# Scan of four head pairs: token buffers in two head layouts, and modulation panels in four column groups

## The chip, the cores and the metric

The kernel runs on one core of a Trainium2 chip. The metric is the device time of one execution in microseconds; the median of three runs is given, and one execution was recorded by the hardware profiler. The core's engines work side by side and meet at semaphores: PE (matmuls; PEld are its weight loads), DVE (VectorE), ACT (ScalarE), POOL (GpSimd), and SP, which issues the loads.

## What is computed

The reference is two transformer blocks on 512 tokens of width 1024. The first mixes tokens with a retention group and an RWKV-7 group (8 heads of 64), then has a mixture of experts; the second has dilated attention, a gated convolution and MLPs. The change lies in the RWKV group of the first block:

```
def rwkv7_scan(r, w, k, v, a, b, s0):
    def step(S, inp):
        r_t, w_t, k_t, v_t, a_t, b_t = inp
        sa = jnp.einsum('bhvk,bhk->bhv', S, a_t)
        S = S * w_t[:, :, None, :] + sa[..., None] * b_t[:, :, None, :] + v_t[..., None] * k_t[:, :, None, :]
        return S, jnp.einsum('bhvk,bhk->bhv', S, r_t)
...
yc_f, sc_f = rwkv7_scan(rc, wc_f, kc, vc, ac, bc, s0)
yc_b, sc_b = rwkv7_scan(*[flip(t) for t in (rc, wc_b, kc, vc, ac, bc)], s0)
y_f, _ = rwkv7_scan(r, w_f, k, v, a, b, sc_f)
y_b, _ = rwkv7_scan(*[flip(t) for t in (r, w_b, k, v, a, b)], sc_b)
lat = g_f * (rwkv_group_norm(y_f, lnx_w, lnx_b) + bonus) + g_b * (rwkv_group_norm(flip(y_b), lnx_w, lnx_b) + bonus)
```

It runs forwards and backwards, over 256 context tokens and then the 512 tokens. The modulation vectors `silu(c) @ w_mod + b_mod` are needed later and are computed in the same stretch.

## The kernel before

The scan is done in blocks of 64 tokens (`CH`), NB = 12 blocks (4 of context, 8 of the rest), so that the step-by-step recurrence becomes 64x64 products. `rwkv_scan` (L1470) runs four times, once for each pair of heads; "scan 1" to "scan 4" below are these. Head 0 of the pair lies on partitions 0 to 63, head 1 on 64 to 127. For each direction d (0 forwards, 1 backwards) the work is a row of named jobs, `pe_jobs`; one job is 24 products (2 heads x 12 blocks) in float32, each written as one call that becomes two weight loads and two matmuls, so 48 matmuls. `both_heads` (L1534) gives the order: head 0 and head 1 in turn, into different PSUM banks. Since a head's inputs and its outputs lie on the same 64 partitions, a job uses the quarter of the array with rows and columns 0 to 63 and the one with rows and columns 64 to 127.

The jobs: SB, SK, SR are scores; KT, BT, AT, V turn an operand; MT is the masked SB, to which an identity is added on DVE (L1738, L1740), M0 its transpose on PE (L1600); AKV is a product. Then come the solver's levels: T1, M1, N1, T2, ... N3, T4, (AT), N4. T multiplies a mask level E (POOL, L1870) by M; ACT copies T out; M and N multiply by T, and DVE adds them to M and MT (L1759). N(lv) needs T(lv), not M(lv). After them XA, XV, ZA, ZV, YA, YV (products, L1552), G, H, RP, and the ten state steps S1 to S10 (L1668 on PE, L1780 on DVE), each of which needs the one before; Y is the output. PE runs a job for d = 0, then for d = 1, then the next job. Three PSUM regions of two banks go round over the list `turns`: a job first waits for the eviction of the job three turns earlier (`bank_free`). KT, M0, BT, AKV, T, AT, XA, XV, ZA, ZV, Y are emptied by ACT (L1826), the rest by DVE; both take orders strictly in the order written.

Between the jobs stand pieces of other work: `RwkvPrep` prepares the next pair (scans 1 to 3; on DVE after MT, N1, N2, N3, N4), and `RwkvOut` finishes the previous pair (scans 2 to 4): `sums` after AT, `square_sums` after ZA, `gates` after YA on PE, and `finish` (L1398) on DVE after YV, seven operations of 512 columns that wait for one another. `ModPanels` (L1412) makes a quarter of the modulation panels of the second half in each scan: 4 panels x 8 slices = 32 units. A unit multiplies a slice of `silu` (2 columns) by 256 columns of weights as two products of 128 columns in two column groups (partitions 0 and 64 of the output, L1435). Eight units stand between RP and S1, the other 24 between the state steps. `keep` (ACT) and `transpose` (PE, after the first Y) bring them into place.

Of the kernel before, what the change touches and what calls it, by code (L numbers as in the profile page):

```python
# [21 lines left out]
ALU = mybir.AluOpType  # L22
# [3 lines left out]
P = 128  # L26
# [1299 lines left out]
class RwkvOut:  # L1326
# [71 lines left out]
    def finish(self, dve):  # L1398

        V, y, step = self.nc.vector, self.y, self.step  # L1400
        for d in range(2):
            dve.wait_ge(self.rooted, d + 1)
            step.link(dve, V.scalar_tensor_tensor(y[:, d], y[:, d], self.col("lnx_w"), self.sq[:, d], ALU.mult, ALU.mult))
            step.link(dve, V.scalar_tensor_tensor(y[:, d], y[:, d], self.col("lnx_b"), self.f.bonus, ALU.add, ALU.add))
            dve.wait_ge(self.gated, d + 1)
            step.link(dve, V.tensor_tensor(y[:, d], y[:, d], self.banks[2][d][:], ALU.mult))
        dst = self.latT[:, 4 + self.hp, :].rearrange("c (j p) -> c p j", j=NT)
        a, b = (y[:, d].rearrange("c (p j) -> c p j", j=NT) for d in range(2))
        step.link(dve, V.tensor_tensor(dst, a, b, ALU.add))


class ModPanels:  # L1412
# [3 lines left out]
    def __init__(self, nc, g, hp, rows, banks):  # L1416
# [8 lines left out]
        self.part = banks[0][0:66].rearrange("r (n c) -> r n c", n=self.n_panel)  # L1425
        self.turn = [b[:, 0:2 * self.n_panel].rearrange("p (n c) -> p n c", c=2) for b in (banks[1], banks[0])]

    def rows_of(self, pe, lo, hi):

        for u in range(lo, hi):  # L1430
# [3 lines left out]
            for i, h in enumerate(self.halves):  # L1434
                last = self.nc.tensor.matmul(self.part[h, n], self.g.silu[:, k, :], self.w[:, k, i * P:(i + 1) * P], start=(k == 0), stop=(k == KD - 1))  # L1435
# [34 lines left out]
def rwkv_scan(nc, g, hp, f, tri, prep_of, out_of):  # L1470
# [20 lines left out]
    pe_jobs = ["SB", "SK", "SR", "KT", "M0", "BT", "AKV", "T1", "M1", "N1", "T2", "M2", "N2", "T3", "M3", "N3", "T4", "AT", "N4",  # L1491
               "XA", "XV", "ZA", "ZV", "YA", "YV", "G", "H", "RP"] + states + ["Y"]
    dve_jobs = ["SB", "SK", "SR", "MT", "M1", "N1", "M2", "N2", "M3", "N3", "N4", "YA", "YV", "G", "H", "RP"] + ["S0"] + states
    act_jobs = ["KT", "M0", "BT", "AKV", "T1", "T2", "T3", "T4", "AT", "XA", "XV", "ZA", "ZV", "Y"]

    with ExitStack() as tmp, nc.Block() as block:
# [23 lines left out]
        mods = ModPanels(nc, g, hp, f.Y[0:66, 1].rearrange("r (n c) -> r n c", c=P), prep_banks)  # L1520
        st, p0 = g.stream, g.stream.taken
        n_unit = KD * mods.n_panel
        turns = [("SB", 0), ("SK", 0), ("SB", 1), ("SK", 1), ("SR", 0), ("KT", 0), ("SR", 1), ("KT", 1), ("V", 0)]
        turns += [(job, d) for job in pe_jobs[4:] for d in range(2)]
        region = {turn: i % 3 for i, turn in enumerate(turns)}
        head = lambda h: slice(HD * h, HD * (h + 1))
# [3 lines left out]
        eye = lambda h: g.ident[head(h), head(h)]  # L1530
        halves = [slice(0, NB // 2), slice(NB // 2, NB)]
# [11 lines left out]

        @block.tensor
        def _(pe):
# [26 lines left out]
            def run(name, d):  # L1572
                bank_free(name, d)
                if name == "SB":
                    for h, s in both_heads(NB // 2):
                        last = mm(cell(d, name, h, s, NB // 2), f.Bh[head(h), d, chunk(s)], f.A[head(h), d, chunk(s)], start=True, stop=True)
# [15 lines left out]
                elif name == "AT":  # L1592
                    dve(d, "N3")
                    last = turn(name, d, f.A[:, d])
                elif name == "M0":
                    dve(d, "MT")
                    if d == 0:
                        pe.wait_ge(v_turned, 1)
                    for h, s in both_heads(NB // 2):
                        last = mm(cell(d, name, h, s, NB // 2), MT[d][head(h), s], eye(h), start=True, stop=True)  # L1600
                elif name == "AKV":
                    act(d, "BT")
                    pe.wait_ge(v_turned, 1)
                    for h, s in both_heads(NB // 2):
                        last = mm(cell(d, name, h, s, NB // 2), AK[d][head(h), s], Vt[head(h), s], start=True, stop=True)
                elif name[0] == "T":
# [6 lines left out]
                    last = product(name, d, E[lv % 2], M)  # L1613
                elif name[0] == "M":
# [6 lines left out]
                    last = product(name, d, MT, T1)  # L1621
                elif name[0] == "N":
# [4 lines left out]
                    last = product(name, d, T1, MT)  # L1627
                elif name == "XA":
                    act(d, "AT")
                    dve(d, "N4")  # L1630
                    last = product(name, d, MT, At)
                elif name == "XV":
                    dve(d, "N4")
                    last = product(name, d, MT, WV)
                elif name == "ZA":
                    pe.wait_ge(pool_done[d], LV)
                    act(d, "XA")
                    last = product(name, d, E[LV % 2], XA)
                elif name == "ZV":
                    act(d, "XV")  # L1640
                    last = product(name, d, E[LV % 2], XV)
                elif name == "YA":
                    act(d, "ZA")
                    last = product(name, d, MT, T1)
                elif name == "YV":
                    act(d, "ZV")
                    last = product(name, d, MT, ZV)
                elif name == "G":
                    dve(d, "YA")
                    last = product(name, d, XA, Bt)  # L1650
# [1977 lines left out]
```

## Time and profile before

| | |
|---|---|
| median of 3 runs | 3154.09 us (3149.6 to 3159.63) |
| the profiled execution | 3149.06 us |
| its span, first to last instruction | 3146.9 us |
| PE busy | 2876.5 us, 91% |
| DVE / ACT / POOL busy | 1134.7 / 942.3 / 778.9 us |
| mean granted TensorE clock | 0.963 |
| scans 1 to 4 (from the first SB to the next scan) | 117.6, 130.9, 131.0, 126.0 us |

In the rows below a time is a start in microseconds from the span's start, then the length. Consecutive instructions of one form are merged into one row (x96 is 96 of them). "idle before <- releaser" is how long the engine had stood still and what ended it; "issue" and "PEq" mean that nothing in the profile but PE's own sequencer was waited for. Some matmul records are missing, so a count may be a few short. A granted clock of 1.00 is 2.4 GHz and 0.50 is 1.2 GHz.

### The profile page before, as it was taken

The page shows a single profiled execution, that of the slowest core. Times are in us where ns is not written, and L with a number is a line of the kernel's source. Part 1 is how long each engine was busy: PE and PEld are TensorE (multiplying, and loading weights), DVE is VectorE, ACT ScalarE, POOL GpSimd, SP SyncE. Part 2 cuts the span into 40 slices and gives each one's busy share as a digit, 9 for nine tenths or more (in the row PEclk, how much of TensorE's full clock was granted, in tenths as well). Part 3 has the DMA queues.
Part 4 walks back from the last instruction along what each step waited for, and adds up shares of the span by engine and source line. Part 5 has one row for each costly group of instructions (what it writes and reads, how often), then busy time and mean ns, then how long its engine had stood idle before and what let it go on. Part 6 is the DMA issues. An engine that isn't in the chain of part 4 may idle for free. (4 is left out here: it accounts for less than half of the span.)

```text
span 3146.9 us, 54449 instructions
## 1 busy us (share of the span) xinstructions
PE 2876.5 (91%) x24397; PEld 2238.6 (71%) x24397; DVE 1134.7 (36%) x1676; ACT 942.3 (30%) x1586; POOL 778.9 (25%) x218
## 2 busy tenths in 40 slices
PE   6987999999967898998899999997999989899998
PEld 4765888887855432333489989986788868678887
DVE  3434764654354300110455447363211123421111
ACT  3123233433323100000235554553322222132221
POOL 3320321220211000000132223222344424334442
PEclk8989999999988899999999999998999999999999
DMA  6111201011122599999521322222232223223321
GB/s 252 54 31 39 67 17 59 4 58 57 45 89 80 216 427 427 427 426 427 224 95 54 81 68 78 70 68 80 69 105 94 94 69 105 69 80 100 102 94 54
DMA packets 171627, 397.57 MB, mean 126 GB/s; under 512 B 9551, under 2 KB 99636, under 8 KB 146036
## 3 DMA queue, kind: packets, MB, share of 16 engines
q1 hardware_dynamic: 170416, 390.70, 33.9%
q8 instruction: 193, 3.16, 0.4%
q10 hardware_dynamic: 980, 3.40, 0.3%
q14 instruction: 38, 0.31, 0.0%
HBM read 387.71 MB, written 4.19 MB: 125 GB/s over the span
## 5 line engine op out<-in xcount | busy, mean ns | idle before, releaser
L179 POOL TENSOR_TENSOR weight_ring_lo<-weight_ring,weight_hi 128x2048 fp32r<-128x2048 f32 (+1 forms) x144 | 657.6, 4568 | 1995.6 <-ACT weight_hi L168 1956.3
L168 ACT CAST weight_hi<-weight_ring 128x2048 fp32r<-128x2048 f32 (+1 forms) x144 | 271.0, 1884 | 671.5 <-PE mlp_o L213 247.3
L213 PE MATMUL a_o<-weight_hi,latT_hi 128*128 128x512 f32 x576 | 176.7, 429 | 2.5 <-PEq L3325 2.5
L213 PE MATMUL a_o<-weight_ring_lo,latT_hi 128*128 128x512 f32 x576 | 158.2, 397 | 0.0
L213 PE MATMUL a_o<-weight_hi,latT_lo 128*128 128x512 f32 x576 | 157.7, 396 | 0.0
L1870 POOL TENSOR_TENSOR rws_E<-rws_AT,rw_tri 128x768 f32<-128x768 f32 x40 | 76.3, 1931 | 322.4 <-DVE rws_AT L1750 209.6
L213 PE MATMUL mlp_o<-weight_hi,mlp_hid_hi 128*128 128x512 f32 x512 | 138.8, 393 | 9.8 <-issue 9.8
L3201 DVE TENSOR_TENSOR x<-x,mlp_o 128x512 f32<-128x512 f32 x64 | 44.0, 687 | 281.4 <-PE mlp_o L213 281.4
L213 PEld LDWEIGHTS a_o<-weight_hi,latT_hi 128*128 128x128 f32 x576 | 133.0, 273 | 16.8 <-issue 8.2
L213 PEld LDWEIGHTS a_o<-weight_ring_lo,latT_hi 128*128 128x128 f32 x576 | 134.2, 270 | 8.1
L213 PEld LDWEIGHTS a_o<-weight_hi,latT_lo 128*128 128x128 f32 x576 | 134.2, 270 | 7.8
L3186 DVE TENSOR_TENSOR mlp_hid<-mlp_hid,mlp_h 128x512 f32<-128x512 f32 x64 | 41.2, 685 | 272.8 <-ACT mlp_hid L3161 272.8
L213 PE MATMUL mlp_o<-weight_ring_lo,mlp_hid_hi 128*128 128x512 f32 x512 | 138.4, 393 | 0.0
L213 PE MATMUL mlp_o<-weight_hi,mlp_hid_lo 128*128 128x512 f32 x512 | 137.1, 390 | 0.0
L204 PE MATMUL mlp_h<-latT_hi,weight_hi 128*128 128x512 f32 x512 | 129.4, 396 | 4.8 <-PEq L3325 4.8
L2405 ACT ACTIVATE moe_silu<-moe_t 128x256 f32<-128x256 f32 x32 | 12.3, 384 | 388.1 <-PE moe_t L2364 387.2
L204 PE MATMUL mlp_h<-latT_lo,weight_hi 128*128 128x512 f32 x512 | 128.3, 393 | 0.0
L204 PE MATMUL mlp_h<-latT_hi,weight_ring_lo 128*128 128x512 f32 x512 | 126.5, 389 | 0.0
L2348 PE MATMUL moe_gu<-weight_ring,moe_xsT 128*64 128x512 f32 x248 | 111.8, 596 | 11.9 <-DMA weight_ring<-in_w_up 6.8
L213 PEld LDWEIGHTS mlp_o<-weight_hi,mlp_hid_hi 128*128 128x128 f32 x512 | 96.9, 190 | 30.6 <-issue 10.5
L2349 PE MATMUL moe_gu<-weight_ring,moe_xsT 128*64 128x512 f32 x256 | 116.2, 598 | 0.0
L204 PEld LDWEIGHTS mlp_h<-latT_hi,weight_hi 128*128 128x128 f32 x512 | 97.6, 191 | 25.7 <-issue 5.4
(617 smaller groups left out, 5801.7 us busy)
## 6 DMA issues: line engine op xcount, KB each, us to landing
weight_ring<-in_mlp_w SPq DMA_DIRECT2D x64, 1024.0 KB, 5.1
weight_ring<-in_a_wqkv SPq DMA_DIRECT2D x36, 1024.0 KB, 5.1
weight_ring<-in_w_up SPq DMA_DIRECT2D x32, 1024.0 KB, 20.3
weight_ring<-in_w_gate SPq DMA_DIRECT2D x31, 1024.0 KB, 22.1
weight_ring<-in_w_down SPq DMA_DIRECT2D x31, 1024.0 KB, 21.6
weight_ring<-in_w_mod SPq DMA_DIRECT2D x24, 1024.0 KB, 5.3
weight_hi_spare<-in_w_up SPq DMA_DIRECT2D x12, 1024.0 KB, 19.9
weight_hi_spare<-in_w_gate SPq DMA_DIRECT2D x12, 1024.0 KB, 22.3
```

The costliest lines, as they stand in the source:

```text
L168: self.nc.scalar.copy(self.view(self.hi[:, q % 2], p, True), self.view(self.slots[self.slot[p]], p, True)).then_inc(self.hi_ready, 1)
L179: self.nc.gpsimd.tensor_tensor(self.view(self.lo[:, s], p, True), self.view(self.slots[s], p, True), self.view(self.hi[:, q % 2], p, True) ...
L204: last = nc.tensor.matmul(dst, left(a, k), right(b, k), start=(a + b + k == 0), stop=(a == 1 and k == KD - 1))
L213: last = nc.tensor.matmul(dst, left(a, HK * r + k), right(b, k), start=(r + a + b + k == 0), stop=(r == 1 and a == 1 and k == HK - 1))
L1870: nc.gpsimd.tensor_tensor(E[lv % 2][d][:], AT[d][:], tri[:, 2 + lv, d].unsqueeze(1).to_broadcast([P, NB, CH]), ALU.mult).then_inc(pool_don ...
L2348: x = nc.tensor.matmul(acc[e % 2][h][0:CAP, :], xsT[:, k, tokens], wg[:, r, cols(h)], start=(k == 0), stop=(k == KD - 1))
L2349: y = nc.tensor.matmul(acc[e % 2][h][CAP:P, :], xsT[:, k, tokens], wu[:, r, cols(h)], start=(k == 0), stop=(k == KD - 1))
L2405: nc.scalar.activation(silu[:, i], turn[i][:, :, 0:CAP], ACT.Silu).then_inc(silued, 1)
L3186: last = V.tensor_tensor(d, d, up[i % 2][h][:], ALU.mult)
L3201: last = V.tensor_tensor(d, d, acc[j][:], ALU.add)
```

## The change

Four things are done.

1. Each 64x64 buffer of a pair is kept in one of three layouts, given as (partition half, slot) for head h and block s: `own` (as before), `left` (head on its own half, blocks of even and odd number in different slots) and `right` (blocks of odd number on the other head's half). With left inputs a product can write a right output and the reverse, so that of four neighbouring products each uses another quarter of the array (`four_tiles`). This holds for M0, AKV, T1 to T4, M1 to M3, AT, XA, XV, ZA, ZV, YA, YV. N1 to N4 and SB stay with two quarters (`two_tiles`), and so do SK, SR, KT, BT, V, G, H, RP and Y in the old order.
2. MT needs the right layout, so SB's products are made a second time, in that layout, as a new job SM; DVE masks them from PSUM instead of from the copy in SBUF. SB0, SB1, SM0, SM1, SK0, SK1 is the new order at the head. M0 no longer waits for Vt.
3. `finish` is split: one of its seven operations follows each of the state steps S1 to S7 on DVE. `gates` moves from after YA to after YV.
4. A mod unit becomes four products of 64 columns in four column groups (output partitions 0, 32, 64, 96), into the unused second bank of the state steps' region. Four units follow each of S1 to S4 and S7 to S10; none stands before S1. ACT copies four pieces instead of two.

```
-    def finish(self, dve):
+    def finish(self, dve, i):
...
+        V, step, d = self.nc.vector, self.step, i // 3
+        if i:
+            step.settle(dve)
...
-            for i, h in enumerate(self.halves):
-                last = self.nc.tensor.matmul(self.part[h, n], self.g.silu[:, k, :], self.w[:, k, i * P:(i + 1) * P], start=(k == 0), stop=(k == KD - 1))
+            for i in range(4):
+                last = self.nc.tensor.matmul(self.part[32 * i:32 * i + 2, n], self.g.silu[:, k, :], self.w[:, k, i * HD:(i + 1) * HD],
+                                             start=(k == 0), stop=(k == KD - 1))
...
-        for h in self.halves:
-            last = self.nc.scalar.copy(self.rows[h], self.part[h])
+        for i in range(4):
+            last = self.nc.scalar.copy(self.rows[self.halves[i // 2], :, HD * (i % 2):HD * (i % 2 + 1)], self.part[32 * i:32 * i + 2])
...
+        mods = ModPanels(nc, g, hp, f.Y[0:66, 1].rearrange("r (n c) -> r n c", c=P), bank[region["S1", 1]][1], prep_banks)
...
+        own = lambda h, s: (h, s)
+        left = lambda h, s: (h, NB // 2 * (h ^ s & 1) + s // 2)
+        right = lambda h, s: (h ^ s & 1, NB // 2 * h + s // 2)
+        at = lambda x, row, s: x[head(row), s]
...
+        def four_tiles():
+            for s in range(0, NB, 2):
+                yield 0, s
+                yield 1, s
+                yield 0, s + 1
+                yield 1, s + 1
+
+        def two_tiles(first):
+            for s in range(0, NB, 2):
+                yield 0, s
+                yield 1, s
+            for s in range(1, NB, 2):
+                yield first, s
+                yield 1 - first, s
...
-            def product(name, d, left, right):
-                for h, s in both_heads(NB // 2):
-                    last = mm(cell(d, name, h, s, NB // 2), left[d][head(h), s], right[d][head(h), s], start=True, stop=True)
+            def product(name, d, x, xs, y, ys, outs, cells):
+                for h, s in cells:
+                    last = mm(cell(d, name, *outs(h, s), NB // 2), at(x[d], *xs(h, s)), at(y[d], *ys(h, s)), start=True, stop=True)
...
-                    last = product(name, d, E[lv % 2], M)
+                    last = product(name, d, E[lv % 2], left, M, left, right, four_tiles())
...
-                    last = product(name, d, MT, T1)
+                    last = product(name, d, MT, right, T1, right, left, four_tiles())
...
-                    last = product(name, d, T1, MT)
+                    last = product(name, d, T1, right, MT, right, right, two_tiles(0))
...
-                elif out and job == "YA":
+                elif out and job == "YV":
                     out.gates(pe)
-                elif job == "RP":
-                    if out:
-                        pe.wait_ge(out.step.sem, 7)
-                    elif prep:
-                        pe.wait_ge(prep.bonus_kept, 1)
-                    mods.rows_of(pe, 0, KD)
-                elif job[0] == "S":
-                    n, left = int(job[1:]), n_unit - KD
-                    mods.rows_of(pe, KD + left * (n - 1) // len(states), KD + left * n // len(states))
+                elif job in states[0:4]:
+                    n = states.index(job)
+                    mods.rows_of(pe, 4 * n, 4 * n + 4)
+                elif job in states[-4:]:
+                    n = states[-4:].index(job) + 4
+                    mods.rows_of(pe, 4 * n, 4 * n + 4)
...
-                if name == "MT":
-                    own("SB")
-                    step.link(dve, V.tensor_tensor(MT[d], AT[d][:], mask(2, d, NB), ALU.mult))
+                if name == "SM":
+                    dve.wait_ge(pe_done[d], pe_jobs.index(name) + 1)
+                    for b, c in enumerate(halves):
+                        step.mark(V.tensor_tensor(MT[d][:, c], part(d, name, b), mask(2, d, NB // 2), ALU.mult))
+                    step.settle(dve)
...
-                elif out and job == "YV":
-                    out.finish(dve)
+                elif out and job in states[0:7]:
+                    out.finish(dve, states.index(job))
```

## Rows read from the trace of the kernel before

**Rows 1.** The page's first line.
```profile
span 3146.9 us, 54449 instructions
```

**Rows 2.** The windows view, scans 1 to 4: window, length, then busy per engine.
```profile
core 0: us, PE busy (x) PEld busy (x) DVE busy (x) ACT busy (x) POOL busy (x), PEclk, DMA share, GB/s
406.50:524.10 117.60, 114.83 (x3218) 105.73 (x3219) 66.58 (x121) 43.03 (x88) 27.66 (x14) 0.98 0.12 39
524.10:655.00 130.90, 121.79 (x3230) 108.48 (x3230) 72.46 (x131) 48.69 (x94) 26.98 (x14) 0.97 0.11 36
...
786.00:912.00 126.00, 115.43 (x3195) 105.43 (x3191) 50.40 (x105) 34.71 (x71) 17.97 (x10) 0.97 0.19 64
```

**Rows 3.** The timeline of scan 4: T1, M1's add, T2, its copy, T4.
```profile
811.73 3.00 PE L1552 MATMUL rws_q<-weight_hi_spare,rws_E 64*64 64x64 f32 x96
...
816.18 1.02 DVE L1759 TENSOR_TENSOR weight_hi_spare<-weight_hi_spare,rws_q 128x384 f32<-128x384 f32 x2 [11.66 <-PE rws_q L1552]
...
820.13 3.00 PE L1552 MATMUL rws_q<-weight_hi_spare,rws_E 64*64 64x64 f32 x96
...
821.77 0.86 ACT L1826 COPY rws_AK<-rws_q 128x384 f32<-128x384 f32 x2 [6.14 <-PE rws_q L1552]
...
837.58 3.02 PE L1552 MATMUL rws_q<-weight_hi_spare,rws_E 64*64 64x64 f32 x94
```

**Rows 4.** The timeline of scan 4 from XA to the second state step, and Y.
```profile
848.14 3.00 PE L1552 MATMUL rws_q<-weight_hi_spare 64*64 64x64 f32 x96
...
866.22 1.96 PE L1370 MATMUL rws_p<-rw_gl,rw_rk 128*128 128x512 f32 x4 [1.82 <-DVE rw_rk L1396]
...
872.11 0.75 DVE L1403 SCALAR_TENSOR_TENSOR rw_Y<-rw_Y,cols,rw_rk 128x512 f32<-128x512 f32 x1
...
877.77 2.84 DVE L1768 TENSOR_TENSOR weight_hi_spare<-rws_q,rw_tri 64x384 f32<-64x384 f32 x5
880.09 0.49 PE L1655 MATMUL rws_q<-rws_E,rws_Bt 64*64 64x64 f32 x4 [3.26 <-DVE weight_hi_spare L1768]
...
887.61 1.92 PE L1435 MATMUL rws_p<-weight_ring,c_silu 128*2 128x128 f32 x32
...
889.45 0.66 PE L1668 MATMUL rws_q<-rws_E,weight_hi_spare 128*128 128x64 f32 x4
...
890.58 0.66 PE L1668 MATMUL rws_q<-rws_E,weight_hi_spare 128*128 128x64 f32 x4
...
901.56 0.32 PE L1674 MATMUL rws_q<-rws_RB,rws_E 64*64 64x64 f32 x2
```

**Rows 5.** The windows view of H's second direction; the last columns are clock and DMA.
```profile
879.80:885.60 5.80, 5.51 (x102) 5.52 (x104) 3.47 (x7) 0.00 (x0) 0.00 (x0) 0.50 0.01 3
```

**Rows 6.** The timeline of SR's first matmuls in scan 1, two quarters in turn.
```profile
416.01 0.27 PE L1585 MATMUL rws_q<-rw_R,rw_Bh 64*64 64x64 f32 x1
...
416.12 0.22 PE L1585 MATMUL rws_q<-rw_R,rw_Bh 64*64 64x64 f32 x1
416.12 0.22 PE L1585 MATMUL rws_q<-rw_R,rw_Kh 64*64 64x64 f32 x1
416.18 0.22 PE L1585 MATMUL rws_q<-rw_R,rw_Bh 64*64 64x64 f32 x1
```

**Rows 7.** The timeline of scan 1: T1; DVE beside POOL in level 3; XA.
```profile
438.51 3.01 PE L1552 MATMUL rws_q<-weight_hi_spare,rws_E 64*64 64x64 f32 x96
...
458.22 4.34 POOL L1870 TENSOR_TENSOR rws_E<-rws_AT,rw_tri 128x768 f32<-128x768 f32 x2 [2.30 <-PE rws_q L1552]
458.58 2.31 DVE L1312 TENSOR_TENSOR rw_rk<-rw_rk,weight_ring 128x512 f32<-128x512 f32 x1
...
460.82 1.77 DVE L1319 TENSOR_TENSOR rw_pe<-rw_pc,rw_pn 128x12 f32<-128x12 f32 x1
...
473.69 2.50 PE L1552 MATMUL rws_q<-weight_hi_spare 64*64 64x64 f32 x79
```

**Rows 8.** The timeline of scan 4, its first job SB.
```profile
785.17 1.61 PE L1576 MATMUL rws_q<-rw_A,rw_Bh 64*64 64x64 f32 x48 [0.99 <-PEq L1496]
```

**Rows 9.** The timeline inside SR of scan 4.
```profile
795.35 0.21 PE L1585 MATMUL rws_q<-rw_rk,rw_Kh 64*64 64x64 f32 x1 [1.34 <-issue]
```

More of the change, by code:

```diff
@@ L1573, in run @@
                 bank_free(name, d)
-                if name == "SB":
-                    for h, s in both_heads(NB // 2):
-                        last = mm(cell(d, name, h, s, NB // 2), f.Bh[head(h), d, chunk(s)], f.A[head(h), d, chunk(s)], start=True, stop=True)
+                if name in ("SB", "SM"):
+                    outs, cells = (left, two_tiles(1)) if name == "SB" else (right, four_tiles())
+                    for h, s in cells:
+                        last = mm(cell(d, name, *outs(h, s), NB // 2), f.Bh[head(h), d, chunk(s)], f.A[head(h), d, chunk(s)], start=True, stop=True)
                 elif name == "SK":
@@ L1593, in run @@
                     dve(d, "N3")
-                    last = turn(name, d, f.A[:, d])
+                    for h, s in four_tiles():
+                        last = mm(cell(d, name, *right(h, s), NB // 2), f.A[head(h), d, chunk(s)], eye(h), start=True, stop=True)
                 elif name == "M0":
[L1596 to L1600, printed above, removed]
+                    dve(d, "SM")
+                    for h, s in four_tiles():
+                        r, i = right(h, s)
+                        last = mm(cell(d, name, *left(h, s), NB // 2), at(MT[d], r, i), eye(r), start=True, stop=True)
                 elif name == "AKV":
@@ L1603, in run @@
                     pe.wait_ge(v_turned, 1)
-                    for h, s in both_heads(NB // 2):
-                        last = mm(cell(d, name, h, s, NB // 2), AK[d][head(h), s], Vt[head(h), s], start=True, stop=True)
+                    for h, s in four_tiles():
+                        last = mm(cell(d, name, *right(h, s), NB // 2), AK[d][head(h), s], Vt[head(h), s], start=True, stop=True)
                 elif name[0] == "T":
@@ L1659, in run @@
                     for h, s in both_heads(NL // 2):
-                        last = mm(cell(d, name, h, s, NL // 2), XA[d][head(h), NBC + s], RB[d][head(h), s], start=True, stop=True)
+                        last = mm(cell(d, name, h, s, NL // 2), at(XA[d], *left(h, NBC + s)), RB[d][head(h), s], start=True, stop=True)
                 elif name[0] == "S":
@@ L1677, in run @@
                 last.then_inc(pe_done[d], 1)
-            for d in range(2):
-                run("SB", d)
-                run("SK", d)
+            for job in pe_jobs[0:3]:
+                for d in range(2):
+                    run(job, d)
             if prep:
@@ L1690, in _ @@
             last.then_inc(v_placed, 1)
-            for job in pe_jobs[4:]:
+            for job in pe_jobs[5:]:
                 if prep and job == "BT":
@@ L1786, in _ @@
                     run(job, d)
[L1787 removed]
+                if prep and job == "SR":
                     prep.squares(dve)
@@ L1915, in _ @@
             out.variance(dve)
-            out.finish(dve)
+            for i in range(7):
+                out.finish(dve, i)
 def project_rows(nc, g, name, part, x, norm_of, x_after=None, xn=None, junk=None, begun=None):
```

62 lines of the change are left out of this document (34 added, 28 removed).

## The prediction

> **What bounds the kernel now.** I read first the page's head for the span [rows 1], then the four windows of the scans. They cover 505.5 us of the 3146.9, and PE is busy there 92 to 98% of the time at a clock near 1 [rows 2]. The page's chain ends in the MLP and says nothing on the scans, but everything behind them waits for them: what the scans lose or win moves the end by as much (the loads behind them start when they end). Then I read the order of work in the fourth scan. One job for one direction is 48 matmuls (24 products of two matmuls each). T1 for both directions starts at 811.73 and T2 at 820.13: six jobs in 8.40 us, 1.40 us each, 29.2 ns per matmul, with PE never waiting [rows 3]. ACT empties a job in 0.86 us and DVE in 1.02, both inside the other direction's 1.40, so **PE sets the pace of the solver levels**. It does not at the tail of a scan: there PE waits for gates (1.82), then 3.26 us for G's bank, and runs H at half clock afterwards [rows 4, 5].
>
> **What a matmul in another quarter costs.** The trace has no job in four quarters. It has two at a time: two matmuls start in the same hundredth (416.12), and the next pair 0.06 later [rows 6]. So the quarters start together and each is busy 58.3 ns with a 64-column matmul; the issue of the second cost under 10 ns. Four quarters would then give 4 matmuls per 58.3 ns, 14.6 each, a job of 0.70 us; no overlap of the new pairs gives 1.40. I take 0.70, since the mod matmuls (32 in 1.92 us, two column groups over all rows) show the column halves running together as the pair above shows the row halves [rows 4].
>
> **Latencies for the walk.** From the last matmul's start to the consumer 0.24 us (T2 820.13 + 1.40 to ACT 821.77), and 0.10 to 0.15 back to PE (DVE's chain of M and N; I take 0.15) [rows 3].
>
> **Levels (T, M, N, three times).** T and M take four quarters, N keeps two. T of both directions 0 to 1.40. ACT empties the first 0.95 to 1.81, so M starts at 1.96, not at 1.40; the second M at 2.82, after ACT's second copy; N runs 3.52 to 6.32. Banks are free in time (N's second DVE add ends at 7.59, that is 1.27 into the next level). A level takes 6.32 instead of 8.40 and not the 5.60 of PE's own work: ACT's turn-round is next late. 2.08 x 3 = 6.2 us in the fourth scan. The Trainium skill, TensorEngine Tiling (Array Packing), section PSUM Bottleneck, warns that evacuation may become the bound after tiling; by PE's work alone a level would be 5.60, and the walk from the rows gives 6.32.
>
> **Levels beside the next pair's preparation (scans 1 to 3).** DVE carries 3.6 to 5 us of preparation per level, and an SBUF-to-SBUF operation waits until POOL's current one is over: 512 elements took 2.31 us while POOL ran, the next, of 12 elements, took 1.77 [rows 7]. Now DVE needs 4.1 + 4 to 5 us in a level that PE leaves after 6.32. Walking it: M2's add waits for the key norm to 11.85, T3 starts at 14.04 instead of 12.64, N3 of the second direction waits for M3's add until 22.2 and T4 starts at 23.6. XA starts 29.5 us after T1 in scan 1 (no sums there), where it was 473.69 - 438.51 = 35.2 [rows 7]: 5.7 saved. If the key norm falls behind POOL too it is 1.5 less; I take 4.2 for each of the three.
>
> **T4, AT, N4 in scan 4.** 837.58 to 848.14 was 10.56 [rows 3, 4]. Now 1.40, a wait to 1.42, 1.40, the head sums 2.0, N4 2.8 of which the second direction overlaps XA: 7.82. Saved 2.7.
>
> **Front.** SM adds two jobs and two evictions; MT's mask from AT goes. M0 and AKV save 1.4 each, M0 no longer waits about 1.0 for Vt. But SK's second direction and SR wait for SM's region, and its add is SBUF to SBUF beside POOL's masks, so SR starts 9.2 to 10.1 after SB instead of 7.3. Net, 1.8 saved of the fourth scan's 785.17 to 811.73 [rows 3, 8], 1.5 in the others.
>
> **XA to S1.** It was 848.14 to 889.45, 41.3 us [rows 4]. Now: XA 0, second direction at 1.40 (it waits for N4's second add), XV to 3.50, ZA 3.5 to 4.9, ACT squares 4.93 to 6.1, square sums 5.7 to 7.6, ZV to 9.1, YA to 10.5, YV to 11.9. YA and YV no longer wait behind gates. Gates wait for the variance (DVE 13.35) and end at 14.7. G 14.7 to 17.5, H 17.5 to 23.1, RP to 25.0. DVE has G at 16.35 to 20.9 (8 x 0.57), so H's bank is free at 18.6, before H's second direction wants it at 20.3: the 3.26 us wait goes, and the half clock behind it with it (5.2 us for 96 matmuls at 0.50, 2.8 at full [rows 5]). The finish operations (5.6 us, 872.11 to 877.73) are gone from here, and so are the 8 mod units between RP and S1 (1.8 us). S1 starts at 26.4. **Saved 14.9**, in scans 2 and 3 the same (15.0). Scan 1 has no outputs to finish: its XA to S1 of 29.3 becomes 21.7, 7.6 saved.
>
> **The ten state steps.** Before: one step is 1.13 us with two mod units (889.45 to 890.58), and 0.22 more with three; 12.1 in scan 4, to Y at 901.56 [rows 4], and 13.1 in scan 1, read the same way. A mod unit (four matmuls; eight units stood in 1.92 us [rows 4], 0.22 each) becomes 8 matmuls of 64 columns in four column groups: 0.12 if all four run together, else 0.22. With four units a step is 1.14 on PE. DVE now has its two state updates (0.51) and one finish operation (0.75, 0.69 or 1.03) per step, about 1.30 for seven steps, 9.3; the last three 1.14. Together 12.7: 0.6 **lost** in scan 4, 0.1 gained in 2 and 3. The finish is thus hidden under steps that were bound by latency. Scan 1 has no finish: 8 x 1.14 + 2 x 0.92 = 11.0 for 13.1, 2.1 saved. The panel for S7 has five steps to land in, as its slot is free after S2; at no step do I see a transfer late. The copies of the mod rows are four instead of two on ACT, under Y's 2.8 us.
>
> **Sum.** Scan 1: 1.5 + 4.2 + 7.6 + 2.1 = 15.4. Scans 2 and 3: 1.5 + 4.2 + 15.0 + 0.1 = 20.8 each. Scan 4: 1.8 + 6.2 + 2.7 + 14.9 - 0.6 = 25.0. Together 82. Against it stands PE's **supply** of instructions: it ran dry at 795 for 1.34 us with "issue" as its releaser, at the old density [rows 9], and where four-quarter jobs follow one another it must be twice as dense. I charge one such stall more per scan, 5.4, and 1.6 for the clock in places where PE now waits (N3 in scans 1 to 3, the steps without mod units): in the trace a wait of 3.26 us was enough to halve it. That leaves 75. From the profiled execution's 3149.1 (span 3146.9) it gives 3074; the median of the three runs is 3154.1, so the same kernel reads up to 5 us higher, and I say 3076.
>
> **Rivals.**
> A. As above. 3076, and 3050 to 3100 by the walk's own looseness (supply and clock between nothing and twice 7; DVE's blocking by POOL between 0 and 3 us per scan; the two unknowns of the mod units, 1 to 3 us per scan).
> B. **The supply is the pace.** The matmuls reach the array no faster than a rate between the 29.2 ns seen and the 14.6 wanted; at 22 ns a job is 1.05 us. Per scan the 16 old pairs of jobs then keep about half of their saving, and what came from moving the finish, gates and mods stays: half-way between A and C, 3100. For it: the stall of [rows 9], and that no stretch of the trace is denser than 29.2. Against it: pairs start within 0.01 us. The Trainium skill, TensorE: Matmul & The Clock Gate, section "Wait — 56ns, not 53.3ns?", states that start-to-start never drops below about 25 ns; the 0.00 to 0.01 us between the starts of a pair disagrees for different quarters, and by it as a sustained rate a job would be 1.2 us and the time an estimated 3108.
> C. **The new quarters don't overlap**: the change doesn't do what it says. A job stays 1.40. What is left is the tail: gates 1.8, H's wait and slow clock about 6, the mods 1.8, the Vt wait 1.0, less SM's 2.8: 7 us in each of scans 2 to 4 and some 1.5 in the first, 22, so 3128. For it: no row shows two column halves of one row half with 64 rows.
> D. **Changing quarters costs.** At the start of a job the second pair comes 0.11 us after the first, not 0.06 [rows 6]. If four_tiles pays part of that at every change between its two diagonals, a pair takes longer than with two quarters. At 0.08 per pair a job is 1.94 us; 34 such jobs in 4 scans, + 0.54 x 136 = 73 on C: 3201. It decides from 0.065 per pair (C's 22 us shared by 136 jobs is 0.16 per job, 1.56 us): above this the kernel is slower than before. Against it: the delay is seen once per job and not in the 32 mod matmuls, which change column groups each time.
>
> **Chances.** A 0.66, B 0.17, C 0.10, D 0.05, something else 0.02. The range reaches over A and B: 3048 to 3118; C and D stay out. A measurement of this kernel tells about 0.3% (9 us) from no change; A, B and C lie beyond it. Faster 0.93, same 0.03, slower 0.04.
>
> **What the profile after would show.** A: T's 96 matmuls in about 1.4 us plus a gap of half a microsecond before M; levels 6.3 us apart in scan 4; no idle before L1655's successor; S1 26 us after XA; DVE nearly without idle between T2 and T4 in scans 1 to 3. B: "issue" as the releaser inside T, M, ZV, YA, and pairs of T at 2.1 to 2.4 us. C: T's 96 in 2.8. D: longer than 2.8. What would make me wrong elsewhere: a half clock through the state steps, since PE has little to do there; each half-clock stretch of 7 us costs up to 3.5.

## The result, and the profile after

The changed kernel takes 3117.87 us (median of 4 runs, 3112.12 to 3126.0) beside 3153.64 for the kernel before in the same rounds: ratio 0.9891, 95% interval 0.9873 to 0.9909. That is 36 us faster. I had said 3076; the time lies at the very upper end of my range (3118), and less than half of the forecast gain is there. One execution of a later version (3378.87 us at a granted clock of 0.795, beside 3091 to 3103 us for its five others) is left out of the comparisons below.

The page's first line and the windows of the four scans (window, length, busy per engine, clock, DMA), after. They answer to [rows 1] and [rows 2]:

```profile
span 3111.1 us, 56253 instructions
...
408.00:522.72 114.72, 95.24 (x3442) 85.89 (x3443) 66.60 (x123) 42.18 (x90) 29.21 (x14) 0.98 0.12 41
522.72:641.76 119.04, 102.15 (x3454) 89.22 (x3455) 75.92 (x133) 47.98 (x97) 29.18 (x14) 0.96 0.13 40
641.76:758.19 116.43, 102.28 (x3455) 89.92 (x3455) 74.59 (x135) 48.02 (x96) 28.44 (x14) 0.94 0.13 41
758.19:873.20 115.01, 91.43 (x3437) 82.64 (x3437) 50.32 (x106) 34.12 (x73) 19.43 (x10) 1.00 0.20 69
```

There are 1804 instructions more, nearly all on PE: 448 per scan (192 for SM, 256 for the mod units). PE was busy 92 to 98% of a scan and is now busy 79 to 88%. So it is no longer its own work that fills the time. What it waits for stands in the view of waits, restricted to PE's weight loads in the scans (line, what released it: us in total, times, longest). Before:

```profile
PEld rws_q L1576 <- issue: 10.5, 6, 4.8
PEld rws_q L1552 <- issue: 10.3, 16, 0.8
PEld rws_q L1655 <- DVE weight_hi_spare L1768: 10.2, 3, 3.4
```

and after, where L1583 is the line of the products (L1552 before):

```profile
PEld rws_q L1583 <- issue: 55.8, 60, 2.1
PEld rws_q L1608 <- issue: 9.5, 5, 4.8
PEld rws_q L1627 <- issue: 5.2, 3, 1.9
```

10.3 us of "issue" have become 55.8, while H's wait for its bank (the L1655 row) is gone. What such a wait looks like is seen in the timeline of PE in scan 4, T1, M1, N1 and the begin of T2. It answers to [rows 3], where the same jobs stood in unbroken rows of 96:

```profile
785.74 1.61 PE L1583 MATMUL rws_q<-weight_hi_spare,rws_E 64*64 64x64 f32 x93
787.71 0.56 PE L1583 MATMUL rws_q<-rws_AK,weight_hi_spare 64*64 64x64 f32 x20 [0.36 <-issue]
789.02 1.32 PE L1583 MATMUL rws_q<-rws_AK,weight_hi_spare 64*64 64x64 f32 x75 [0.75 <-issue]
790.14 0.23 PE L1583 MATMUL rws_q<-weight_hi_spare,rws_AK 64*64 64x64 f32 x2
790.19 0.22 PE L1583 MATMUL rws_q<-rws_AK,weight_hi_spare 64*64 64x64 f32 x1
790.19 1.62 PE L1583 MATMUL rws_q<-weight_hi_spare,rws_AK 64*64 64x64 f32 x49
793.02 1.50 PE L1583 MATMUL rws_q<-weight_hi_spare,rws_AK 64*64 64x64 f32 x44 [1.21 <-issue]
794.30 0.27 PE L1583 MATMUL rws_q<-weight_hi_spare,rws_E 64*64 64x64 f32 x2
794.35 0.22 PE L1583 MATMUL rws_q<-weight_hi_spare,rws_AK 64*64 64x64 f32 x1
794.36 1.44 PE L1583 MATMUL rws_q<-weight_hi_spare,rws_E 64*64 64x64 f32 x80
796.90 0.29 PE L1583 MATMUL rws_q<-weight_hi_spare,rws_E 64*64 64x64 f32 x4 [1.10 <-issue]
```

Read it in two steps. First, the four quarters do run together: 93 matmuls of T1 start within 1.61 - 0.22 = 1.39 us, 15 ns each, as forecast. (The Trainium skill, TensorE: Matmul & The Clock Gate, section "Wait — 56ns, not 53.3ns?", states that start-to-start never drops below about 25 ns. This burst of different quarters disagrees.) Second, count from one long stop to the next. From 789.02 to 793.02 there are 75 + 2 + 1 + 49 = 127 matmuls, from 793.02 to 796.90 again 44 + 2 + 1 + 80 = 127. With their weight loads that is 254 instructions, each time, in 4.00 and 3.88 us: 65 per us. The matmuls come in bursts and stop whenever some 256 instructions have been used up. Before, the dense jobs used 2 per 29.2 ns, 68.5 per us [rows 3]: the kernel already ran at the edge of this **supply**, and its 1.34 us stall [rows 9] may be one of the places where that showed (another, of 0.63 us, stands inside SB at 789.13).

Scan 4 by windows from its stages' starts (same columns): T1 to H, H to S1, S1 to Y; and S1 to Y of scan 3. Before:

```profile
811.70:873.80 62.10, 60.28 (x1846) 56.05 (x1842) 22.27 (x43) 25.38 (x49) 10.81 (x6) 1.00 0.02 4
873.80:889.50 15.70, 12.44 (x295) 11.78 (x289) 11.99 (x23) 0.00 (x0) 0.00 (x0) 0.78 0.01 2
889.50:901.60 12.10, 12.10 (x139) 8.70 (x137) 5.07 (x20) 0.00 (x0) 0.00 (x0) 1.00 0.70 235
763.30:776.10 12.80, 12.29 (x138) 8.56 (x136) 5.07 (x20) 0.00 (x0) 0.00 (x0) 1.00 0.70 232
```

After:

```profile
785.70:841.90 56.20, 43.79 (x1846) 37.91 (x1841) 21.58 (x43) 22.11 (x46) 10.84 (x6) 1.00 0.02 5
841.90:850.90 9.00, 7.87 (x264) 7.74 (x259) 6.98 (x16) 2.64 (x4) 0.00 (x0) 1.00 0.02 4
850.90:862.00 11.10, 10.39 (x296) 8.74 (x296) 9.36 (x27) 0.00 (x0) 0.00 (x0) 1.00 0.59 200
734.20:749.50 15.30, 13.79 (x296) 11.47 (x296) 9.88 (x27) 0.00 (x0) 0.00 (x0) 0.72 0.59 196
```

H to S1 went from 15.70 us at clock 0.78 to 9.00 at 1.00. S1 to Y takes 11.1 us at clock 1.00, but 15.3 in scan 3, where the clock was 0.72. Windows of this kind, summed over the four scans, give the account that the rest of the text uses (us; for the last scan "Y to next" ends with Y's last matmul; the experiments are told below):

| kernel | SB to T1 | T1 to H | H to S1 | S1 to Y | Y to next |
|---|---|---|---|---|---|
| before | 118.8 | 242.6 | 56.7 | 50.7 | 33.0 |
| changed | 116.8 | 220.3 | 36.2 | 53.0 | 36.9 |
| changed, order of two quarters | 120.6 | 222.9 | 36.3 | 53.6 | 34.5 |
| tail alone | 120.6 | 237.6 | 36.0 | 57.4 | 33.4 |
| changed, second execution | 116.3 | 222.6 | 36.0 | 56.8 | 39.0 |
| order of two quarters, second execution | 121.8 | 223.7 | 36.6 | 57.2 | 35.8 |
| before, T split | 121.1 | 288.0 | 53.6 | 51.0 | 33.2 |
| changed, T split | 118.3 | 265.3 | 36.5 | 55.8 | 35.9 |
| 128-column products | 114.3 | 200.9 | 36.0 | 62.1 | 36.8 |
| the same, old mod units | 115.9 | 203.1 | 36.0 | 57.7 | 31.6 |
| the same, old mod units over all ten steps | 116.2 | 204.5 | 36.0 | 65.7 | 32.0 |
| changed, old mod units over all ten steps | 116.2 | 221.4 | 36.0 | 60.8 | 32.1 |
| order of two quarters, old mod units | 123.9 | 224.4 | 36.0 | 57.8 | 32.4 |

### The profile page after: what moved, and what is told of

It reads as the page before. It is cut to its first block and busy times, and to the rows that moved or that the text cites. A ratio compares the mean times of both kernels' runs of the same rounds, so it can differ in the third digit from the quotient of the medians.

```text
span 3111.1 us, 56253 instructions
## 1 busy us (share of the span) xinstructions
PE 2800.3 (90%) x25293; PEld 2160.5 (69%) x25293; DVE 1140.3 (37%) x1684; ACT 939.6 (30%) x1594; POOL 785.9 (25%) x218
## 5 line engine op out<-in xcount | busy, mean ns | idle before, releaser
L1905 POOL TENSOR_TENSOR rws_E<-rws_AT,rw_tri 128x768 f32<-128x768 f32 x40 | 83.3, 2104 | 287.8 <-DVE rws_AT L1785 186.9
L2384 PE MATMUL moe_gu<-weight_ring,moe_xsT 128*64 128x512 f32 x248 | 111.7, 596 | 12.9 <-DMA weight_ring<-in_w_up 7.3
L213 PEld LDWEIGHTS mlp_o<-weight_hi,mlp_hid_hi 128*128 128x128 f32 x512 | 96.9, 190 | 30.6 <-issue 10.5
L2385 PE MATMUL moe_gu<-weight_ring,moe_xsT 128*64 128x512 f32 x256 | 116.2, 598 | 0.0
```

What stands on the lines that cost most here:

```text
L213: last = nc.tensor.matmul(dst, left(a, HK * r + k), right(b, k), start=(r + a + b + k == 0), stop=(r == 1 and a == 1 and k == HK - 1))
L1905: nc.gpsimd.tensor_tensor(E[lv % 2][d][:], AT[d][:], tri[:, 2 + lv, d].unsqueeze(1).to_broadcast([P, NB, CH]), ALU.mult).then_inc(pool_don ...
L2384: x = nc.tensor.matmul(acc[e % 2][h][0:CAP, :], xsT[:, k, tokens], wg[:, r, cols(h)], start=(k == 0), stop=(k == KD - 1))
L2385: y = nc.tensor.matmul(acc[e % 2][h][CAP:P, :], xsT[:, k, tokens], wu[:, r, cols(h)], start=(k == 0), stop=(k == KD - 1))
```

## The experiments

Two theories stood against each other. **Supply**: PE gets some 65 to 75 instructions per us on average, whatever they do, so time is paid per instruction. **Quarters**: time is paid by what the array does, and the missing gain went elsewhere.

**1. The changed kernel in the order of two quarters.**

```
         def four_tiles():
-            for s in range(0, NB, 2):
-                yield 0, s
-                yield 1, s
-                yield 0, s + 1
-                yield 1, s + 1
+            yield from two_tiles(0)
```

> The changed kernel with one edit: the order of products in every four-quarter job is that of the two-quarter ones (first the two quarters in turn for the even blocks, then the other two for the odd ones), so a 64x64 job never has more than two quarters busy. Layouts, SM, the split finish, gates and mod units stay; the number of instructions is the same. Theory S, supply: PE's instructions reach it at no more than about 70 per us (two per 29.2 ns in rows 3), whatever quarter they use; a two-quarter job of 1.40 us is already at that rate, so this costs little: 3118 to 3130 us, a T pair 2.8 us without idle before it instead of 1.67 us with idle of 1 to 3 us. Theory Q, quarters: the four quarters do save their 0.70 us per job (34 jobs in each of 4 scans, 95 us, some half of it on the path) and the missing gain was eaten by a fixed loss elsewhere, such as DVE behind POOL: 3160 to 3175 us.

Measured: 3122.67 us (3113.86 to 3130.82), ratio 0.9913, interval 0.9898 to 0.9928. Once more, beside the unedited changed kernel in the same rounds:

> The changed kernel in the order of two quarters, once more and in the same rounds as the changed kernel: what the four quarters are worth alone. Theory S: 2 to 8 us, for a burst at 14.6 ns per matmul is paid back by the stall after it. Theory Q: over 40 us.

> The changed kernel itself, unedited, on the same chip and in the same rounds as the two above, so that it stands beside them directly: 3112 to 3126 us, as before. Theory S puts it 2 to 8 us below the version in two quarters with the same units (3122.7 us).

Measured: 3128.67 (ratio 0.9925, 0.9911 to 0.9938) against 3121.57 (0.9908, 0.9894 to 0.9922). By the medians the order of four quarters is worth some 5 to 7 us of the 29 to 36 (the intervals of the two ratios overlap), most of it between SB and T1; theory Q wanted over 40. In one point my expectation was wrong: this kernel's T pair doesn't take 2.8 us. The timeline of PE, T1 of scan 4:

```profile
788.27 2.33 PE L1579 MATMUL rws_q<-weight_hi_spare,rws_E 64*64 64x64 f32 x91
790.55 0.80 PE L1579 MATMUL rws_q<-rws_AK,weight_hi_spare 64*64 64x64 f32 x20
791.95 1.81 PE L1579 MATMUL rws_q<-rws_AK,weight_hi_spare 64*64 64x64 f32 x70 [0.60 <-issue]
```

91 starts in 2.11 us are 23 ns each, not 29.2. The two diagonals of the array follow each other inside a job, and where one ends and the next begins, the trace has four starts within 0.02 us. So this order, too, asks for more than the supply gives, and stalls, only less.

**2. The tail alone.** The kernel before, with `finish` split over S1 to S7, gates after YV and the mod units moved, in their old form. No layouts, no SM.

```
-                elif out and job == "YA":
+                elif out and job == "YV":
                     out.gates(pe)
...
-                    mods.rows_of(pe, 0, KD)
-                elif job[0] == "S":
-                    n, left = int(job[1:]), n_unit - KD
-                    mods.rows_of(pe, KD + left * (n - 1) // len(states), KD + left * n // len(states))
+                elif job in states[0:4]:
+                    n = states.index(job)
+                    mods.rows_of(pe, 4 * n, 4 * n + 4)
...
-                elif out and job == "YV":
-                    out.finish(dve)
+                elif out and job in states[0:7]:
+                    out.finish(dve, states.index(job))
```

> The kernel before with only its tail changed: finish split over S1 to S7 on DVE, gates after YV, mod units (old form, two products of 128 columns) four after each of S1 to S4 and S7 to S10, none before S1. No SM, no layouts, two quarters as before, 448 PE instructions fewer per scan than the changed kernel. Theory S: nearly all that the change gained comes from the tail, and SM with the longer mod units costs what the quarters bring: 3110 to 3128 us. Theory Q: the tail is 22 us of my forecast, and less if it was over-estimated like the rest: 3132 to 3145 us.

Measured: 3136.39 us, ratio 0.9958 (0.9946 to 0.9971), 14 us for the tail. That lies in Q's range and not in S's: the layouts and the order do bring more than the SM and the units cost, and "nearly all from the tail" was wrong. Why this doesn't speak for the quarters is seen in the stretch T1 to H. The account of this kernel: H to S1 20.7 us less, T1 to H 5.0 less, S1 to Y 6.7 more. Its window T1 to H in scan 4 shows PE without a pause:

```profile
801.60:861.30 59.70, 59.70 (x1844) 55.74 (x1840) 21.65 (x42) 23.63 (x47) 10.80 (x6) 1.00 0.02 4
```

With the same number of matmuls PE is busy for 59.70 us here and for 43.79 in the changed kernel, but that one's stretch is 56.20 long. The kernel before had two limits side by side: the quarters (58.3 ns per matmul in each) and, with a stretch 6% shorter (56.2 for 59.7 us), the supply. My S expected this kernel to be at the supply already; it is at the quarters. An order that alternates the diagonals lifts the first limit, and the second is hit at once.

**3. Twice the instructions for the same columns.** Each product of T1 to T4 as two of 32 columns, in the kernel before and in the changed one:

```
...
+                    for c in (slice(0, CH // 2), slice(CH // 2, CH)):
+                        last = mm(dst[:, c], left[d][head(h), s], right[d][head(h), s, c], start=True, stop=True)
...
```

> The kernel before, each product of T1 to T4 made as two products of 32 columns: the same columns in the same quarters, but eight instructions instead of four, 768 more per scan. Theory S: each instruction costs about 14.3 ns (1 / 70 per us), 11 us per scan, 44 in all: 3190 to 3205 us, and a T pair takes 5.5 us instead of 2.8. Theory Q: the array has the same columns to do: 3154 to 3165 us.

> The changed kernel, each product of T1 to T4 made as two of 32 columns, 768 PE instructions more per scan, in four quarters. In the kernel before the same edit cost 47 us, but there either the supply (14.6 ns per instruction) or a fixed 58.3 ns per matmul in its quarter could explain it. Here four quarters share the load: a job's 96 matmuls need 1.40 us of quarters and 192 instructions of supply. Theory S: 14 to 15 ns each, +43 to +47 us, 3161 to 3166 us. Theory Q (58.3 ns per matmul in a quarter, supply not binding): 0.70 us more per job, 8 jobs in each of 4 scans, +22 us, 3140 us.

Measured: 3197.29 us (ratio 1.0147, 1.0134 to 1.0160), 47 more than the kernel before, and 3164.27 (1.0035, 1.0022 to 1.0048), 46 more than the changed kernel (43 more than its second measurement). Per added instruction that is 15.3 and 14 to 15 ns. In the kernel before it looks like this (timeline of PE, T1 and M1 of scan 4):

```profile
849.61 5.87 PE L1555 MATMUL rws_q<-weight_hi_spare,rws_E 64*64 64x32 f32 x192
855.29 3.01 PE L1557 MATMUL rws_q<-rws_AK,weight_hi_spare 64*64 64x64 f32 x96
```

A matmul of 32 columns takes as long as one of 64, 29.4 ns in two quarters, with no idle time: by this row alone the quarter could be the cause as well. The changed kernel decides it:

```profile
824.49 1.92 PE L1585 MATMUL rws_q<-weight_hi_spare,rws_E 64*64 64x32 f32 x113
828.20 1.24 PE L1585 MATMUL rws_q<-weight_hi_spare,rws_E 64*64 64x32 f32 x69 [1.80 <-issue]
...
829.38 1.69 PE L1585 MATMUL rws_q<-rws_AK,weight_hi_spare 64*64 64x64 f32 x49
831.83 1.44 PE L1585 MATMUL rws_q<-rws_AK,weight_hi_spare 64*64 64x64 f32 x42 [0.77 <-issue]
```

There the array does 113 matmuls in 1.7 us and then stands still for 1.80; Q's 3140 is off by 24 us, S's 3161 to 3166 holds. Between 828.20 and 831.83 there are again 69 + 1 + 4 + 2 + 2 + 49 = 127 matmuls (the short rows left out carry the 9), in 3.63 us. The page's part on DMA queues counts packets of a kind named instruction (packets, MB, share); in order the kernel before, the same with T split, the changed kernel, the same with T split:

```profile
q8 instruction: 193, 3.16, 0.4%
```
```profile
q8 instruction: 205, 3.36, 0.4%
```
```profile
q8 instruction: 200, 3.28, 0.4%
```
```profile
q8 instruction: 212, 3.47, 0.5%
```

3072 instructions more are 12 packets more, 256 to a packet: the size of the bursts. The trace also has the time of each of these packets of 16 KB. Around the stops of the changed kernel in scan 4 that were counted out above:

| packet starts | packet has landed | PE goes on | next packet starts |
|---|---|---|---|
| 786.74 | 787.70 | 789.02 | 790.27 |
| 790.27 | 791.59 | 793.02 | 794.16 |
| 794.16 | 795.52 | 796.90 | 798.14 |

PE goes on 1.3 to 1.4 us after a packet has landed, and the next packet starts 1.1 to 1.3 us after PE goes on. This holds beyond scan 4. Of the waits of PE's weight loads in the four scans that were longer than 0.8 us and ended by "issue", 35 of 38 ended 1.1 to 1.6 us after such a landing (36 of 41 in the second execution, 40 of 42 with T split); a moment picked at random would do so in 12% of cases, and before the change 2 of 14 did. Shorter stops, as the one that ended at 787.71, don't all follow this. So the long stops are waits for the next 256 instructions. In the table the packets start 3.5 to 4.0 us apart, 3.8 in the mean: 256 / 3.8 = 67 instructions per us. In all scans of all the kernels no two started closer than 3.2 us. What fills the time between a landing and PE's next instruction is not shown.

**4. Fewer instructions for the same columns.** If time is paid per instruction, the pairs XA and XV, ZA and ZV, YA and YV, whose weights are the same, can be made together:

```
...
+            def pair(name, d, x, xs, y, ys, outs):
+                half = NB // 2
+                for h, s in four_tiles():
+                    if (s >= half) != (name[1] == "V"):
+                        continue
+                    r, i = outs(h, s)
+                    b, c = i // half, (i % half - half // 2 * (name[1] == "V")) * 2 * CH
+                    q, j = ys(h, s)
+                    last = mm(bank[region[name, d]][b][head(r), c:c + 2 * CH].rearrange("p (a t) -> p a t", t=CH), at(x[d], *xs(h, s)),
+                              y[d][head(q), :, j], start=True, stop=True)
+                return last
...
```

> The changed kernel, complete, with XA and XV, ZA and ZV, YA and YV made together: they have the same weights, so one product of 128 moving columns (A part and V part side by side) replaces two of 64. Each job now does half of the blocks for both parts. The columns and the PSUM evictions stay, 144 products = 576 PE instructions per scan go. Theory S (supply, 1 instruction per 14 to 15 ns: the split T jobs cost 47 us for 3072 instructions, 15.3 ns each): up to 8.1 us per scan, 32 in all, less where ACT's copies (8 of 0.86 us per pair of jobs) come to bound the chain; I expect 6 us per scan, 3094 us, 3086 to 3105. Theory Q (array or evictions bound these jobs): 3112 to 3125 us.

Measured: 3097.81 us (median of five), ratio 0.9818 (0.9803 to 0.9832): 20 us faster than the changed kernel by the medians, 23 by the ratios, so supply is confirmed in its direction and in most of its size (24 expected). The count of instruction packets went from 200 to 191, 9 x 256 = 2304 instructions fewer, as written. T1 to H lost 19.5 us, 4.9 per scan. In its timeline of PE, scan 4, X and Z:

```profile
812.09 2.20 PE L1600 MATMUL rws_q<-rws_ZZ,weight_hi_spare 64*64 64x128 f32 x72 [0.51 <-DVE weight_hi_spare L1803]
814.07 1.52 PE L1600 MATMUL rws_q<-rws_XX,rws_E 64*64 64x128 f32 x48
```

72 matmuls in 1.98 us, 27.5 ns each. This row alone doesn't speak for the supply: inside it four matmuls start every 109 to 110 ns, so each quarter takes 110 ns for 128 columns where it took 58.3 for 64, and four quarters at work come to 27.5 ns as well. In these jobs the quarters and the supply (two instructions per 27.5 ns, 73 per us) are limits of the same size; it is the total, with Q at 3112 or more, that decides. Only part of the 8.1 us per scan came, and "issue" still is the largest wait of its levels (31.0 us). More was lost further on: S1 to Y became 9.1 us longer, because of the clock. Its windows of these steps in scans 4 and 3:

```profile
836.60:850.70 14.10, 13.40 (x297) 11.17 (x297) 9.74 (x27) 0.00 (x0) 0.00 (x0) 0.75 0.62 212
722.40:739.40 17.00, 16.75 (x296) 14.00 (x296) 10.21 (x27) 0.00 (x0) 0.00 (x0) 0.56 0.53 175
```

**5. The mod units and the clock.** Four kernels with the old form of a unit, two products of 128 columns. First the changed kernel and the 128-column version, with the units spread over all ten steps; then the 128-column version and the two-quarter order, with the units in the changed kernel's places:

```
-            for i in range(4):
-                last = self.nc.tensor.matmul(self.part[32 * i:32 * i + 2, n], self.g.silu[:, k, :], self.w[:, k, i * HD:(i + 1) * HD],
-                                             start=(k == 0), stop=(k == KD - 1))
+            for i, h in enumerate(self.halves):
+                last = self.nc.tensor.matmul(self.part[h, n], self.g.silu[:, k, :], self.w[:, k, i * P:(i + 1) * P], start=(k == 0), stop=(k == KD - 1))
...
```

> The changed kernel with mod units in their old form, two products of 128 columns in two column groups, spread over all ten state steps (three or four each): 256 PE instructions fewer per scan, longer array time per unit. Theory S: up to 256 x 14.3 ns = 3.7 us per scan less, nothing where PE waits for DVE anyway: 3103 to 3115 us. Theory Q: four column groups are the better form, 0.14 to 0.16 us a unit against 0.22, so this is 2 to 3 us per scan slower: 3125 to 3130 us.

> As the one with 128-column products, and with the mod units in their old form of two products over all ten state steps (another 256 instructions fewer per scan). The changed kernel with that edit alone came to 3123 us, no faster, since PE waits for DVE in the state steps. If instructions cost only where PE would otherwise not wait: same as the merged one within 6 us. If the supply runs ahead in the state steps and the fewer instructions there help what follows: 5 to 10 us faster than the merged one.

> The version with 128-column products, with one edit: a mod unit is again two products of 128 columns in two column groups, in the same places (four after each of S1 to S4 and S7 to S10). In the merged version the four stretches from S1 to Y took 14.0, 16.9, 17.0 and 14.1 us at a granted clock of 0.79, 0.56, 0.56 and 0.75, and Y to the next scan 36.8 us in all at 0.78 to 0.89; with the tail alone, whose units are of this form, they took 14.2 to 14.4 us at 1.00, and 33.4 in all. Theory clock: the half clock follows from PE doing too little in these steps, the wider units keep it up: 57.4 for 62.0 and 33.4 for 36.8, 8 us less, 3091 us, clock 1.00 from S1 to Y. Theory units: the four column groups halve a unit, so the wider ones cost their 0.1 us x 32 per scan: 12 us more, 3111 us.

> The changed kernel in the order of two quarters, and with the mod units of two products of 128 columns in the changed kernel's places. Against the one with the tail alone (3136 us) it has only the layouts, SM, the mask on SB from PSUM and the alternation of the two diagonals; against the one with two quarters (3123 us) only the form of the mod units. If the form of the units were what lies between these two (13.7 us), it comes to 3136 us. If it is the rest, that is the stretch from T1 to H (53.8 to 57.4 us there, 55.8 to 61.1 with the tail alone): S1 to Y goes from 53.6 us in four scans to 57.4, Y to the next scan from 34.5 to 33.4, so 3125 us, and 3121 to 3129.

Measured, in this order: 3123.27 (ratio 0.9918, 0.9905 to 0.9931), 3101.96 (0.9834, 0.9821 to 0.9847), 3094.81 (0.9818, 0.9805 to 0.9831) and 3124.24 (0.9905, 0.9890 to 0.9921). In the first, 256 instructions fewer per scan bring nothing: they lie in the state steps, where PE's instructions are not what is waited for (S1 to Y took 60.8 us at clock 1.00, 7.8 more than with narrow units at a falling clock), so S's 3103 to 3115 was wrong there, and Q's 3125 to 3130 as well, if by little. The second is within the 6 us expected. The third kept the clock, as its windows S1 to Y of scans 4 and 3 show:

```profile
830.10:844.50 14.40, 13.70 (x168) 10.34 (x168) 9.64 (x27) 0.00 (x0) 0.00 (x0) 1.00 0.57 179
718.80:733.20 14.40, 13.71 (x169) 10.32 (x169) 9.63 (x27) 0.00 (x0) 0.00 (x0) 1.00 0.57 185
```

In these places and at full clock the ten steps take 14.2 to 14.8 us with wide units and 11.1 to 13.3 with narrow ones, but with narrow ones the clock was mostly lower, and then they took 13.2 to 17.1. S1 to Y and Y to next are together 9.6 us shorter than in experiment 4, close to the 8 expected, but T1 to H and SB to T1 are 3.8 longer in this execution, and the ratio is the same 0.9818. So the clock is regained and the time hardly: that the wide units cost as much elsewhere is not shown, the account of one execution is too coarse for it. In the same rounds the changed kernel took 3121.57, so this version is 27 us faster than it. The fourth came as expected and shows that the form of the units is not what separates the changed kernel from the tail alone: 3124 against 3136, with the same units. What separates them is the stretch T1 to H (224.4 against 237.6 us), where only layouts and order differ; SM's price is seen in SB to T1, 123.9 against 120.6.

## Why the prediction was wrong, step by step

- **Four quarters take 0.70 us per job**: right inside a burst, 15 ns per matmul, and wrong as a lasting pace. Rivals C and D fall.
- **PE sets the pace of the levels**: right for the kernel before, and the sum built on it failed at the term for **supply**. I had its one stall [rows 9] and charged one more per scan, 5.4 us. The account shows 242.6 - 220.3 = 22.3 us saved from T1 to H, where my steps (levels 18.8, T4 to N4 2.7, XA to H 31.4) make 52.9: 30.6 short. SB to T1 is another 4.3 short (2.0 for 6.3), where SM's 192 instructions alone are 2.9 us per scan at 15 ns. In the changed kernel's four stretches T1 to H PE stood still for 47.9 us, and of the 68.6 us that its weight loads waited there 65.6 ended by "issue", 1.1 by ACT's copies. Rival B named the mechanism and sized it wrongly: it took 22 ns per matmul, between 14.6 and 29.2. In truth 2 instructions cost about 30 ns on average, which is what the kernel before already used; a burst may be fast, but it is followed by the stop that makes up for it. The dense row of [rows 3], 68.5 instructions per us, was not a sign of room but close to the ceiling, and I had no row that let rival B run faster than that for long.
- **ACT's turn-round, DVE behind POOL, N3 of the second direction**: my walk of the levels has them; they can't be judged, since the stalls of PE hide them. Some sums in it are off by a little: the parts given for T4 to N4 add to 7.6 and not 7.82 us, scan 1's steps before took 12.9 and not 13.1, and rival C's parts make 7.8 and not 7 us per scan. None of these decides anything.
- **The tail**: right. H to S1 was forecast at 26.4 - 17.5 = 8.9 us and is 9.0 to 9.2 in all scans; the bank wait went and the half clock with it. The tail alone gives 20.7 us there, and 5.0 in T1 to H for the gates (5.4 forecast).
- **The state steps**: 11.1 us in scan 4 at full clock, where I had 12.7 and the kernel before 12.1. The four column groups do run together, and DVE's finish operations fit. But scans 2 and 3 fell to clocks of 0.78 and 0.72 and took 14.3 and 15.3. S1 to Y and Y to next lost 2.3 + 3.9 us where I had forecast a gain of 1.7 and a clock loss of 1.6. I had named this as what would make me wrong, and priced it too low. In the second execution of the changed kernel the four stretches were 14.1, 16.9, 14.8 and 11.1 us: how much is lost differs from one execution to the next.
- **The sum**: forecast 82 - 7 = 75, measured 38.6 in the account of the scans (35.8 in the spans). Of the 43.4 between 82 and 38.6, 30.6 + 4.3 lie where the supply is the limit (no run parts them from what the walk of the levels may have had wrong besides), 7.9 lie in the steps and Y, mostly the clock's, and 0.6 in H to S1. That 3117.87 is still inside 3048 to 3118 is luck: the sum was 42 us off, and the range reached so far only because it took in rival B. Of the 36 us, some 14 are the tail's (experiment 2) and some 20 come from the layouts and the order.

## What to carry to other kernels

Before you make small matmuls faster, divide the instructions of the densest stretch by its time, weight loads counted. Here the kernel before ran its levels at 68.5 per us, and the changed one, with faster jobs, got 65.6 per us from T1 to H of scan 4 (3687 in 56.2 us). Over a short time more is possible, from what has been fetched ahead: up to 124 per us over 4 us and 86 over 12 us in the changed kernel. At the lasting rate, a faster array brings only stalls, and an edit that adds instructions (a second copy of a job, products cut into columns) costs 15 ns each. What helps is more columns per instruction: the same columns in fewer and wider products gave 20 to 27 us on top (the 27 with wide mod units as well).

## What the runs showed of the hardware

- PE's instructions came in packets of 16 KB for 256 instructions, started 3.2 us apart at the closest. Where PE used them at once, one block lasted 3.6 to 4.0 us; within a block bursts of 15 ns per matmul with its weight load. PE went on 1.1 to 1.6 us after the landing in 35 of the 38 long stops of the changed kernel.
- Matmuls of 64 rows and 32 columns started no faster than those of 64 columns: 29.4 and 29.2 ns apart in two quarters, 15 ns in bursts over four. Of 128 columns in four quarters, one started every 27.5 ns, 110 ns per quarter.
- In the order of two quarters the change from one diagonal of the array to the other cost nothing: four matmuls started within 0.02 us there, and T1's came every 23 ns on average.
- The granted clock from S1 to Y was 1.00 in all scans of all traces with wide units (128 columns) but one (0.77, scan 1 of the 128-column version with spread units), and 0.55 to 0.96 in 18 of the 24 scans with narrow ones, also where a kernel was run twice.
